# A two-block transformer kernel in one program: the third attention loop's output copies behind the exponentials, and two fill steps between scores and value products

## The chip, the cores and the metric

One core of one Trainium2 chip. The time is the device time of one execution in microseconds, for all of the work from the inputs in HBM to the output in HBM. The program is written with explicit queues: each engine (TensorE, VectorE, ScalarE, GpSimd, and SyncE for loads) has its own list of instructions, which it executes in order, and semaphores between them.

## The reference, cut to what matters

256 tokens, 1024 features, fp32. Block one (a latent and a grouped attention, an MLP, a gated embedding) and then two layers, of which the first has gated linear attention and an attention with forgetting, and the second the attention that this change touches. Each layer has two gated feed-forward halves.

```python
def odd_mixer(h, w_in, kv_norm_g, w_uk, w_uv, w_out, t5_table):
    q, ckv, q_idx, k_idx, w_idx = jnp.split(h @ w_in, ODD_SPLITS, axis=-1)
    c = rmsnorm_2(ckv, kv_norm_g)
    q_lat = jnp.einsum('bshd,hdl->bshl', q.reshape(B, S, DSA_HEADS, DSA_DH), w_uk)
    o_lat = dsa_attention(q_lat, c, ...)     # per query the best k_top keys by an index score
    o = jnp.einsum('bshl,hld->bshd', o_lat, w_uv).reshape(B, S, D_MIX_ODD)
    return o @ w_out
# in dsa_attention, for 16 heads of 64:
    s = q_lat . c_sel * DSA_DH ** -0.5 + bias(distance)      # masked where distance < 0
    p = softmax(s);  o_lat = p . c_sel
```

## The kernel before

**Matrix products.** Weights come in as chunks of 128 x 2048 fp32, in halves of 1024 columns. SyncE loads a half to `raw`; ScalarE copies it rounded to the type of TensorE's operand to `whi` (`split_half`, line 1267); VectorE writes the rest, raw minus rounded, to `wlo` (line 1715). Activations are split in the same way into a high and a low part. A product is three matmuls: high by high, high by low, low by high (`mm3`).

**The third attention loop** (`attention("odd", ...)`, one function per engine, lines 677, 1387 and 1899) works on 16 heads in 8 pairs. It has ten passes, here called rounds 0 to 9; `p` is the round. The keys and values are expanded per head beforehand, and the top-k selection is a mask that is added to the scores, so that each head is a product of 256 queries by 256 keys in two tiles: queries 0 to 127 with keys 0 to 127, queries 128 to 255 with all 256 (`OFF`, `KL`). In round p the engines do this, each in this order:

- TensorE: the scores of pair p to PSUM banks 4 and 5 (`score`, line 467 `pp<-fa`), when VectorE has reduced the pair before (`s_smax`); the value products of pair p-2 to bank 7 (`weigh`, `pp<-ptb,fa`), when ScalarE has copied that pair's turned weights (`s_ptc`) and VectorE has taken the low part of the output before (`s_ols`); fill steps (`fill(p, 0)`); the turning of head 2p-2, by transposes (`turn_weights`, line 476), when VectorE has scaled it (`s_shr`); `fill(p, 1)`; the turning of head 2p-1; `fill(p, 2)`.
- VectorE: for each of the two heads two fused operations (line 1924) that add mask and bias to the scores, write them negated to `xn`, and reduce them to the row's extreme in `st`; the low part of the output of pair p-2 (`out_lo`, line 1715 `ra<-pp,ra`), when ScalarE has written the high part (`s_ohs`); the low parts of weight halves that ScalarE split in the round before (`lows`); evictions of finished fill products (`evict`, line 1723); for each head the reciprocal of its sums (line 1952) and two scalings of the weights in `pbuf` (line 1719), when ScalarE has done the exponentials (`s_ex`).
- ScalarE: the high part of the output of pair p-2 from bank 7 (`out_hi`, line 1403, recorded at line 1267 as `ra<-pp`), when the value products are done (`s_pv`); four exponentials of pair p (line 1418); two copies of the turned weights of pair p-1 (`ptb<-pp`, line 1267); at most one weight half (`one_more`).
- GpSimd: for each head a load of a row of position biases, and two additions of it to the mask (line 2478), when VectorE has reduced the head three before.

A **fill step** is three or six matmuls of a product that has nothing to do with the pair at hand. The steps are q2 (16 steps), q3 (16), which are the queries of pairs 4 to 7, and the output projection's first half oo0.0 and oo1.0 (8 each). How many stand at which of the three places of a round comes from two tables:

```python
STEPS = {...
         "odd": {0: (7, 0, 0), 2: (3, 1, 0), 5: (3, 0, 0), 6: (2, 1, 1), 7: (2, 1, 1), 8: (2, 1, 1)}}
USUAL = {..., "odd": (3, 1, 2)}
```

q2 is thus finished in round 2 and q3 in round 5, both at the first place. VectorE's eviction of q2 (`turned_`, line 2347) is done in round 2 and that of q3 in round 5, each between the weight half and the reciprocals. The scores of round 6 wait for the eviction of q3 (`entry`, `s_qT`). Which weight halves are split in a round is fixed by how far the fill steps have come at the round's end (`ended`, `split_at`).

Of the kernel before, what the change touches and what calls it, by code (L numbers as in the profile page):

```python
# [163 lines left out]
def program(nc, W, XIN, XT, PT_IN, CST, GNS, GQK, GFIN, GFIN2, GLAG, FOXB, T5, OUT):  # L164
# [22 lines left out]
    with ExitStack() as ctx:  # L187
# [3 lines left out]
        def sem(name):  # L191
# [3 lines left out]
        ps = [pp[:, i, :] for i in range(8)]  # L195
# [36 lines left out]
        s_sc, s_smax, s_negm, s_ex, s_rcp, s_shr, s_ptn, s_ptc, s_pv, s_ohs, s_ols = [  # L232
            sem(n) for n in ("s_sc", "s_smax", "s_negm", "s_ex", "s_rcp", "s_shr", "s_ptn", "s_ptc", "s_pv",
                             "s_ohs", "s_ols")]
# [65 lines left out]
        def lo_slot(j):  # L300
# [106 lines left out]
        STEPS = {"first": {0: (9, 0, 0)}, "fox": {0: (12, 0, 0), 4: (6, 3, 3)},  # L407
                 "odd": {0: (7, 0, 0), 2: (3, 1, 0), 5: (3, 0, 0), 6: (2, 1, 1), 7: (2, 1, 1), 8: (2, 1, 1)}}
# [47 lines left out]
        def out_hi(block, j):  # L456
            return oh[:, j, :] if block == "first" else mh[:, 4 + j, :] if block == "fox" else mh[:, j, :]
# [7 lines left out]
        def tensor_program(pe):  # L465
# [211 lines left out]
            def attention(name, entry, extra, units):  # L677
                h0, pairs = HEAD0[name], COUNT[name] // 2
                off, kl = spans(name)
                causal = name != "first"  # L680
                sbk, obk = SB[name], OB[name]

                def fill(p, at):
                    point[0] = (p, at)
                    for _ in range(STEPS[name].get(p, USUAL[name])[at]):
                        next(units, None)

                def score(h, t):
                    return mm(ps[sbk[h % 2]][:, off[t]:off[t] + kl[t]], query(name, h, t), keys(name, h, kl[t]), True, True)

                def weigh(h, k):
                    o = ps[obk[h // 2 % len(obk)]][64 * (h % 2):64 * (h % 2) + 64, 0:256]
                    if causal and k == 1:
                        return mm(o[:, 128:256], values(name, h, 1), ptb[:, h % 2, 256:384], False, True)
                    return mm(o, values(name, h, k), ptb[:, h % 2, 256 * k:256 * k + 256], k == 0, k == 1)

                def turn_weights(h):
                    b = turn_bank(name, h)
                    src = weights_slot(name, h)
                    pe.wait_ge(s_shr, h0 + h + 1)  # L700
                    held = [g for g in range(h) if turn_bank(name, g) == b]
                    if held:
                        pe.wait_ge(s_ptc, h0 + held[-1] + 1)
                    elif name == "first" and b == 3:
                        pe.wait_ge(s_qbe, 3)
                    elif name == "odd" and b == 3:
                        pe.wait_ge(s_kT, 4)
                    elif name == "fox" and b == 3:
                        pe.wait_ge(s_Fout, 1)
                    for t in range(2):  # L710
                        for k in range(kl[t] // 128):
                            c = 256 * k + 128 * (t - k if causal else t)
                            y = tp(ps[b][:, c:c + 128], src[:, off[t] + 128 * k:off[t] + 128 * k + 128])
                    y.then_inc(s_ptn)

                for p in range(pairs + 2):
                    if p < pairs:
                        entry(p)
                        if p and causal:
                            pe.wait_ge(s_smax, 2 * (h0 - 16 + 2 * p))  # L720
                        elif p:
                            pe.wait_ge(s_ex, h0 + 2 * p)
                        if name == "first" and p < 4:
                            for h in (2 * p, 2 * p + 1):
                                score(h, 0)
                                score(h, 1).then_inc(s_sc)
                        else:
                            score(2 * p, 0)
                            score(2 * p + 1, 0)
                            score(2 * p, 1).then_inc(s_sc)  # L730
                            score(2 * p + 1, 1).then_inc(s_sc)
                    if p >= 2:
                        pr = p - 2
                        pe.wait_ge(s_ptc, h0 + 2 * pr + 2)
                        if pr >= len(obk):
                            pe.wait_ge(s_ols, h0 // 2 + pr + 1 - len(obk))
                        weigh(2 * pr, 0)
                        weigh(2 * pr + 1, 0)
                        weigh(2 * pr, 1).then_inc(s_pv)
                        weigh(2 * pr + 1, 1).then_inc(s_pv)  # L740
                    point[0] = (p, 0)
                    late = (name, p) == ("fox", 3)
                    if not late:
                        extra(p)
                    fill(p, 0)
                    if late:
                        extra(p)
                    ended[name, p, 0] = consumed[0]
                    if 1 <= p <= pairs:
                        turn_weights(2 * p - 2)  # L750
                        fill(p, 1)
                        turn_weights(2 * p - 1)
                        fill(p, 2)
                    ended[name, p, 1] = consumed[0]
# [509 lines left out]
        def scalar_program(act):  # L1264
            def copy(o, i, scale=None):
                if scale is None:
                    return act.activation(o, i, ACT.Copy, scale=1.0)  # L1267
                return act.activation(o, i, ACT.Copy, scale=scale)  # L1268
# [118 lines left out]
            def attention(name, evict):  # L1387
                h0, pairs = HEAD0[name], COUNT[name] // 2
                off, kl = spans(name)
                causal = name != "first"  # L1390
                sbk, obk = SB[name], OB[name]
                tot = off[1] + kl[1]

                def one_more(p, at):
                    if next_half[0] < HEND[min(ended[name, p, at] - 1 + NHL, LAST)]:
                        split_half()
                    split_at[name, p, at] = next_half[0]

                for p in range(pairs + 2):
                    if p >= 2:  # L1400
                        pr = p - 2
                        act.wait_ge(s_pv, h0 + 2 * pr + 2)
                        copy(out_hi(name, pr), ps[obk[pr % len(obk)]][:, 0:256]).then_inc(s_ohs)
                    for h in (2 * p, 2 * p + 1) if p < pairs else ():
                        hc = h0 + h
                        nm, sm, rs = head_stats(hc)
                        src = stt[:, h % 2, 0:tot] if causal else ps[sbk[h % 2]][:, 0:tot]
                        if causal:
                            act.wait_ge(s_smax, 2 * (hc - 16) + 2)
                        else:  # L1410
                            act.wait_ge(s_negm, hc + 1)
                        if h >= 4:
                            act.wait_ge(s_ptn, hc - 3)
                        if h >= 8:
                            act.wait_ge(s_shr, hc - 7)
                        o = weights_slot(name, h)
                        for t in range(2):
                            y = act.activation(o[:, off[t]:off[t] + kl[t]], src[:, off[t]:off[t] + kl[t]], ACT.Exp,
                                               bias=nm[:, t:t + 1], scale=-1.0 if causal else 1.0, accum_out=sm[:, t:t + 1])
                        y.then_inc(s_ex)  # L1420
                    evict((name, p, 0))
                    if not causal or p >= pairs:
                        one_more(p, 0)
                    if 1 <= p <= pairs:
                        for par in range(2):
                            h = 2 * p - 2 + par
                            act.wait_ge(s_ptn, h0 + h + 1)
                            if h >= 2:
                                act.wait_ge(s_pv, h0 + h - 1)
                            copy(ptb[:, par, 0:tot], ps[turn_bank(name, h)][:, 0:tot]).then_inc(s_ptc)  # L1430
                            evict((name, p, 1 + par))
                    if name == "fox" and p < pairs:
                        one_more(p, 0)
                    one_more(p, 1)
# [1164 lines left out]
```

## Time and profile before

| | |
|---|---|
| median of 3 runs | 1359.39 us (1357.41 to 1359.88) |
| profiled execution | 1357.3 us, its span 1355.3 us |
| granted TensorE clock, mean | 0.998 |
| TensorE busy (matmuls) | 1337.9 us, 99% |
| TensorE busy (weight loads) | 1147.4 us, 85% |
| VectorE busy | 969.8 us, 72% |
| ScalarE busy | 678.7 us, 50% |
| GpSimd busy | 69.6 us, 5% |

The profile is of one execution. Its times are microseconds from the start of the span; the third attention loop lies between about 1106 and 1151. A share of busy time is a mean over all stages, of which this loop is 3%. A row of a timeline gives the start, the duration, the engine, the line, the operation with its output and inputs and, in square brackets, how long the engine was idle before it and what ended that. A small overlap of successive rows of an engine is usual, as a record includes the end of the write. Where a helper records an operation, rows of many places carry its line (1267, 1715, 467), and the tile's name tells them apart.

### The profile page before, as it was taken

How to read it: one execution, taken by the hardware profiler on the slowest of the kernel's cores; microseconds unless marked ns; L12 is line 12 of the kernel's file. 1: busy time of each engine (PE TensorE's matmuls, PEld its weight loads, DVE VectorE, ACT ScalarE, POOL GpSimd, SP SyncE). 2: the span in 40 equal slices, each digit the busy share in tenths (PEclk: the TensorE clock that was granted, in tenths of full speed). 3: DMA queues.
4: the chain of work that ended last, by engine and by line, in shares of the span. 5: the costliest groups of instructions: out<-in, count | busy, mean ns of one | idle time of the engine just before them, and what ended most of it. 6: DMA issues, size and time to landing. Idle time of an engine off the chain costs nothing.

```text
span 1355.3 us, 19411 instructions
## 1 busy us (share of the span) xinstructions
PE 1337.9 (99%) x7680; PEld 1147.4 (85%) x7680; DVE 969.8 (72%) x1326; ACT 678.7 (50%) x1057; POOL 69.6 (5%) x109
## 2 busy tenths in 40 slices
PE   9999999999999999999999999999999999999998
PEld 6988888888888888898888888888888886888886
DVE  6886677666687777657667777787776798576775
ACT  6586454444554444456554443544443567544442
POOL 0300010000000000004000000000000034000000
PEclk9999999999999999999999999999999999999999
DMA  9353556555546555464446555555554554466551
GB/s 338 114 166 115 182 176 229 186 186 188 185 141 220 198 188 186 156 204 125 147 153 218 187 187 192 178 188 196 193 192 151 182 175 130 146 204 203 186 187 47
DMA packets 67594, 241.31 MB, mean 178 GB/s; under 512 B 7999, under 2 KB 8392, under 8 KB 67504
## 3 DMA queue, kind: packets, MB, share of 16 engines
q1 hardware_dynamic: 65200, 234.19, 51.9%
q0 software_dynamic: 2016, 5.77, 1.7%
q8 instruction: 61, 1.00, 0.3%
q14 instruction: 29, 0.24, 0.1%
q10 hardware_dynamic: 288, 0.11, 0.0%
HBM read 238.88 MB, written 1.09 MB: 177 GB/s over the span
## 4 chain that ended last, share of the span: by engine, by line
PE 86%; DVE 9%; ACT 2%; issue 2%; DMA 1%; POOL 0%; SPq 0%; DVEq 0%; POOLq 0%; ACTq 0%
PE pp L467 84%; DVE wlo L1715 3%; PE pp L476 2%; DVE pbuf L1719 1%; DVE fa L1715 1%; DVE xn L1924 1%; DVE hx L1723 1%; DMA raw<-w_chunks 1%; ACT whi L1267 0%; DVE fa L1815 0%; DVE fa L2294 0%; DVE xn L1715 0%; ACT hx L1268 0%; DVE st L2290 0%; DMA fa<-f_rows 0%
## 5 line engine op out<-in xcount | busy, mean ns | idle before, releaser
L1715 DVE TENSOR_TENSOR wlo<-raw,whi 128x1024 fp32r<-128x1024 f32 (+1 forms) x444 | 522.4, 1218 | 140.3 <-ACT whi L1267 140.0
L467 PE MATMUL pp<-hx,whi 128*128 128x512 f32 (+1 forms) x2400 | 541.1, 360 | 2.1 <-DVE fa L1815 1.3
L1267 ACT ACTIVATE whi<-raw 128x1024 fp32r<-128x1024 f32 (+1 forms) x444 | 441.7, 1043 | 90.6 <-PE pp L467 81.1
L467 PEld LDWEIGHTS pp<-hx,whi 128*128 128x128 f32 x2400 | 419.7, 188 | 74.3 <-issue 8.5
L467 PE MATMUL pp<-whi,ra 128*128 128x512 f32 x1144 | 366.2, 391 | 0.0
L467 PE MATMUL pp<-hx,wlo 128*128 128x256 f32 x2032 | 314.3, 278 | 0.0
L467 PEld LDWEIGHTS pp<-hx,wlo 128*128 128x128 f32 x2032 | 278.4, 188 | 9.9
L467 PEld LDWEIGHTS pp<-whi,ra 128*128 128x128 f32 x1144 | 214.6, 188 | 43.7 <-issue 0.9
L467 PE MATMUL pp<-wlo,ra 128*128 128x512 f32 x572 | 222.7, 389 | 0.0
L1815 DVE TENSOR_REDUCE fa<-pp 128x512 f32<-128x1024 f32 x104 | 126.9, 1220 | 73.4 <-PE pp L467 73.3
L1267 ACT ACTIVATE ra<-fa 128x512 fp32r<-128x512 f32 x63 | 39.8, 632 | 227.9 <-DVE fa L1723 227.9
L1363 ACT ACTIVATE fa<-fa 128x512 f32<-128x512 f32 x44 | 27.8, 632 | 195.1 <-DVE fa L1715 195.1
L467 PEld LDWEIGHTS pp<-wlo,ra 128*128 128x128 f32 x572 | 107.4, 188 | 20.3 <-issue 0.2
L467 PE MATMUL pp<-whi,hx 128*128 128x512 f32 (+2 forms) x320 | 96.0, 376 | 1.9 <-DVE wlo L1715 1.9
L1715 DVE TENSOR_TENSOR ra<-fa,ra 128x512 fp32r<-128x512 f32 x63 | 43.6, 693 | 43.3 <-ACT ra L1267 43.3
L467 PEld LDWEIGHTS pp<-whi,hx 128*128 128x128 f32 x320 | 58.4, 188 | 17.3 <-issue 6.0
L2384 POOL TENSOR_TENSOR st<-st,cst 128x2 f32<-128x2 f32 (+3 forms) x15 | 13.4, 895 | 1162.7 <-DVE st L1720 1162.7
L467 PE MATMUL pp<-wlo,hx 128*128 128x512 f32 (+2 forms) x160 | 59.4, 371 | 0.0
L1723 DVE SCALAR_TENSOR_TENSOR fa<-fa 128x512 f32<-128x512 f32 x65 | 44.4, 683 | 2.8 <-ACT fa L1614 0.7
L1723 DVE SCALAR_TENSOR_TENSOR hx<-pp,gns,hx 128x256 fp32r<-128x256 f32 x64 | 26.5, 477 | 22.9 <-ACT hx L1268 22.9
L1306 ACT ACTIVATE xn<-X 128x512 f32<-128x512 f32 x36 | 22.4, 627 | 28.3 <-DVE X L1723 28.0
L1715 DVE TENSOR_TENSOR fa<-fa,rbb 128x512 f32<-128x512 f32 x47 | 32.4, 691 | 3.5 <-ACT fa L1603 1.1
(175 smaller groups left out, 773.0 us busy)
## 6 DMA issues: line engine op xcount, KB each, us to landing
raw<-w_chunks SPq DMA_DIRECT2D x438, 512.0 KB, 5.2
fa<-t_rows POOLq DMA_DIRECT2D x16, 128.0 KB, 3.4
fx<-x_t SPq DMA_DIRECT2D x2, 512.0 KB, 6.5
X<-x_in SPq DMA_DIRECT2D x2, 512.0 KB, 7.5
fa<-g_fin POOLq DMA_DIRECT2D x2, 512.0 KB, 4.1
fa<-f_rows POOLq DMA_DIRECT2D x8, 128.0 KB, 3.2
raw<-w_chunks SPq DMA_DIRECT2D x3, 256.0 KB, 5.7
cst<-consts POOLq DMA_DIRECT2D x1, 576.0 KB, 7.5
```

Of the source, the lines that this page charges most:

```text
L467: return pe.matmul(o, lhs, rhs, start=first, stop=last, skip_group_check=True)
L476: return pe.transpose(o, src, ident[0:n, 0:n])
L1267: return act.activation(o, i, ACT.Copy, scale=1.0)
L1306: act.activation(xn[:, t, sl], X[:, t, sl], ACT.Square, scale=1.0, accum_out=st[:, q + 2 * c + t:q + 2 * c + t + 1]).then_inc(s_sq)
L1363: act.activation(fr[:, g % 2, :], fr[:, g % 2, :], ACT.Silu, scale=1.0).then_inc(s_silu)
L1715: return dve.tensor_tensor(o, a, b, op)
L1719: return dve.tensor_scalar(o, a, s1, None, op0)
L1723: return dve.scalar_tensor_tensor(out=o, in0=a, scalar=s, in1=b, op0=op0, op1=op1)
L1815: return dve.tensor_reduce(two(o), pp[:, b:b + 2, :].rearrange("p f (s c) -> p f c s", s=2), AX.X, ALU.add)
L1924: dve.tensor_tensor_reduce(out=src[:, sl], in0=bank[:, sl], in1=more[:, sl], scale=-1.0, scalar=-GONE, op0=ALU.add, op1=ALU.min, accum_out ...
L2384: return pool.tensor_tensor(o, a, C("mhalf")[:, 0:1].to_broadcast([128, n]), ALU.pow)
```

## The change

On ScalarE, in the third loop only, the copy of the output's high part (`out_copy`) stands behind the four exponentials of the round instead of ahead of them. On TensorE, in rounds 2 to 7 of the third loop only, the first two of the fill steps at the first place (of two or three) stand between the scores and the value products; the rest stay behind the value products. The other two attention loops keep their order. VectorE, GpSimd and SyncE have the same instructions in the same order.

```diff
-                def fill(p, at):
+                def fill(p, at, skip=0, most=99):
                     point[0] = (p, at)
-                    for _ in range(STEPS[name].get(p, USUAL[name])[at]):
+                    for _ in range(min(most, STEPS[name].get(p, USUAL[name])[at] - skip)):
                         next(units, None)
...
                             score(2 * p, 1).then_inc(s_sc)
                             score(2 * p + 1, 1).then_inc(s_sc)
+                    early = 2 if name == "odd" and 2 <= p < pairs else 0
+                    if early:
+                        fill(p, 0, 0, early)
                     if p >= 2:
                         pr = p - 2
                         pe.wait_ge(s_ptc, h0 + 2 * pr + 2)
...
                     if not late:
                         extra(p)
-                    fill(p, 0)
+                    fill(p, 0, early)
                     if late:
                         extra(p)
...
+                def out_copy(pr):
+                    act.wait_ge(s_pv, h0 + 2 * pr + 2)
+                    copy(out_hi(name, pr), ps[obk[pr % len(obk)]][:, 0:256]).then_inc(s_ohs)
+
                 for p in range(pairs + 2):
-                    if p >= 2:
-                        pr = p - 2
-                        act.wait_ge(s_pv, h0 + 2 * pr + 2)
-                        copy(out_hi(name, pr), ps[obk[pr % len(obk)]][:, 0:256]).then_inc(s_ohs)
+                    if p >= 2 and name != "odd":
+                        out_copy(p - 2)
                     for h in (2 * p, 2 * p + 1) if p < pairs else ():
...
                         y.then_inc(s_ex)
+                    if p >= 2 and name == "odd":
+                        out_copy(p - 2)
                     evict((name, p, 0))
```

TensorE, rounds 3 and 4: `pp<-fa` are the scores, `pp<-ptb,fa` the value products, `pp<-hx,whi` and `pp<-hx,wlo` the matmuls of fill steps, and `pp<-cst,pbuf` the turnings.

```order
 L467 MATMUL pp<-fa 128x128 x2
 L467 MATMUL pp<-fa 128x256 x2
+L467 MATMUL pp<-hx,whi 128x256 x2
+L467 MATMUL pp<-hx,wlo 128x256
+L467 MATMUL pp<-hx,whi 128x256 x2
+L467 MATMUL pp<-hx,wlo 128x256
 L467 MATMUL pp<-ptb,fa 64x256 x2
 L467 MATMUL pp<-ptb,fa 64x128 x2
 L467 MATMUL pp<-hx,whi 128x256 x2
 L467 MATMUL pp<-hx,wlo 128x256
-L467 MATMUL pp<-hx,whi 128x256 x2
-L467 MATMUL pp<-hx,wlo 128x256
```

Six matmuls, two steps, moved ahead of the value products; one step is left behind them, ahead of the first turning.

ScalarE, round 2, before: `ptb<-pp` are the copies of turned weights, `whi<-raw` a weight half, `ra<-pp` the output copy, and the rows of line 1418 the exponentials.

```order
L1267 ACTIVATE ptb<-pp 128x384 x2
L1267 ACTIVATE whi<-raw 128x1024
L1267 ACTIVATE ra<-pp 128x256
L1418 ACTIVATE pbuf,st<-xn,st 128x128
L1418 ACTIVATE pbuf,st<-xn,st 128x256
L1418 ACTIVATE pbuf,st<-xn,st 128x128
L1418 ACTIVATE pbuf,st<-xn,st 128x256
L1267 ACTIVATE ptb<-pp 128x384 x2
L1267 ACTIVATE whi<-raw 128x1024
```

ScalarE, the same round in the changed kernel (its lines 1270 and 1423 are lines 1267 and 1418 of before):

```order
L1270 ACTIVATE ptb<-pp 128x384 x2
L1270 ACTIVATE whi<-raw 128x1024
L1423 ACTIVATE pbuf,st<-xn,st 128x128
L1423 ACTIVATE pbuf,st<-xn,st 128x256
L1423 ACTIVATE pbuf,st<-xn,st 128x128
L1423 ACTIVATE pbuf,st<-xn,st 128x256
L1270 ACTIVATE ra<-pp 128x256
L1270 ACTIVATE ptb<-pp 128x384 x2
L1270 ACTIVATE whi<-raw 128x1024
```

The output copy moved from ahead of the four exponentials to between them and the copies of turned weights. It is so in each of rounds 2 to 7; rounds 8 and 9 have no exponentials.

## Rows read from the trace of the kernel before

**Rows 1.** The page, busy time of each engine with its share of the span.
```profile
PE 1337.9 (99%) x7680; PEld 1147.4 (85%) x7680; DVE 969.8 (72%) x1326; ACT 678.7 (50%) x1057; POOL 69.6 (5%) x109
```

**Rows 2.** The chain of waits from 1116 to 1136, its shares by engine and line.
```profile
by line: DVE pbuf L1719 24.3%; DVE wlo L1715 20.8%; DVE xn L1924 20.0%; issue 8.1%; ACT pbuf L1418 6.9%; PE pp L467 6.5%; DVE ra L1715 5.0%; ACT ptb L1267 3.8%; DVE fa L1723 3.0%; DVE st L1952 2.5%; DVE st L1924 0.6%; DVEq L2347 0.2%; ACTq 
```

**Rows 3.** Busy time of each engine in round 2 (length, then each engine).
```profile
1116.50:1122.30 5.80, 5.51 (x48) 4.62 (x49) 5.73 (x19) 4.31 (x13) 5.02 (x8) 1.00 0.66 210
```

**Rows 4.** Timeline of VectorE, rounds 2 to 5 (start, duration, operation).
```profile
1116.45 0.28 DVE L1924 CUSTOM_DVE_ANT_0 xn<-pp,fa 128x128 f32<-128x128 f32 x1
...
1117.56 0.41 DVE L1715 TENSOR_TENSOR ra<-pp,ra 128x256 fp32r<-128x256 f32 x1
1117.90 1.21 DVE L1715 TENSOR_TENSOR wlo<-raw,whi 128x1024 fp32r<-128x1024 f32 x1
1119.03 0.68 DVE L1723 SCALAR_TENSOR_TENSOR fa<-pp,rbb 128x512 f32<-128x512 f32 x1
...
1120.56 1.75 DVE L1719 TENSOR_SCALAR pbuf<-pbuf,st 128x128 f32<-128x128 f32 x2
1122.23 0.28 DVE L1924 CUSTOM_DVE_ANT_0 xn<-pp,fa 128x128 f32<-128x128 f32 x1
...
1123.68 1.60 DVE L1715 TENSOR_TENSOR wlo<-raw,whi 128x1024 fp32r<-128x1024 f32 x1
...
1125.39 1.04 DVE L1719 TENSOR_SCALAR pbuf<-pbuf,st 128x128 f32<-128x128 f32 x2
...
1131.76 0.28 DVE L1924 CUSTOM_DVE_ANT_0 xn<-pp,fa 128x128 f32<-128x128 f32 x1
...
1133.20 0.68 DVE L1723 SCALAR_TENSOR_TENSOR fa<-pp,rbb 128x512 f32<-128x512 f32 x1
```

**Rows 5.** Timeline of VectorE, rounds 6 to 8.
```profile
1138.84 0.55 DVE L1719 TENSOR_SCALAR pbuf<-pbuf,st 128x128 f32<-128x128 f32 x2
...
1140.49 0.29 DVE L1924 CUSTOM_DVE_ANT_0 xn<-pp,fa 128x128 f32<-128x128 f32 x1 [0.44 <-PE pp L467]
...
1146.35 0.42 DVE L1715 TENSOR_TENSOR ra<-pp,ra 128x256 fp32r<-128x256 f32 x1 [1.73 <-ACT ra L1267]
```

**Rows 6.** Timeline of TensorE's weight loads, rounds 2 to 7.
```profile
1115.53 0.63 PEld L467 LDWEIGHTS pp<-ptb,fa 128*64 128x64 f32 x8 [1.26 <-ACT ptb L1267]
...
1119.79 0.63 PEld L467 LDWEIGHTS pp<-ptb,fa 128*64 128x64 f32 x8 [0.69 <-ACT ptb L1267]
1120.59 0.30 PEld L467 LDWEIGHTS pp<-hx,whi 128*128 128x128 f32 x2 [0.17 <-issue]
...
1121.66 0.35 PEld L476 LDWEIGHTS pp<-cst,pbuf 128*128 128x128 f32 x3
...
1125.57 0.63 PEld L467 LDWEIGHTS pp<-ptb,fa 128*64 128x64 f32 x8 [1.46 <-ACT ptb L1267]
...
1130.35 0.63 PEld L467 LDWEIGHTS pp<-ptb,fa 128*64 128x64 f32 x8 [0.51 <-ACT ptb L1267]
...
1133.93 0.52 PEld L467 LDWEIGHTS pp<-fa 64*128 64x128 f32 x8 [1.03 <-DVE fa L1723]
...
1135.09 0.63 PEld L467 LDWEIGHTS pp<-ptb,fa 128*64 128x64 f32 x8 [0.63 <-ACT ptb L1267]
...
1142.45 0.48 PEld L476 LDWEIGHTS pp<-cst,pbuf 128*128 128x128 f32 x3
```

**Rows 7.** Timeline of ScalarE, round 2 and round 8.
```profile
1117.12 0.40 ACT L1418 ACTIVATE pbuf<-xn,st 128x128 f32<-128x128 f32 x1 [0.26 <-DVE st L1924]
...
1118.90 0.84 ACT L1267 ACTIVATE ptb<-pp 128x384 f32<-128x384 f32 x2
...
1145.95 0.37 ACT L1267 ACTIVATE ra<-pp 128x256 fp32r<-128x256 f32 x1
```

**Rows 8.** Timeline of GpSimd, mask additions in rounds 2 and 3.
```profile
1120.99 1.16 POOL L2478 TENSOR_TENSOR fa<-fa 128x128 f32<-128x128 f32 x2
...
1123.03 1.16 POOL L2478 TENSOR_TENSOR fa<-fa 128x128 f32<-128x128 f32 x2
```

## The prediction

> **What bounds the kernel now.** I read the page first: TensorE is busy 99% of the span [rows 1], so a change must shorten or lengthen one of its few gaps. All instructions that move lie in the third attention loop, some 44 us of the 1355.3. I number its passes as rounds 0 to 9, and use letters: S(p) the scores of pair p and V(p-2) the value products of the pair two back (TensorE), R(p) the four reductions, L the low part of a weight half, N(p) the scaling by the reciprocal sums (VectorE), E(p) the four exponentials, C(p-1) the copies of turned weights, O(p-2) the copy of the output (ScalarE), OL(p-2) the output's low part (VectorE, reads what O wrote).
>
> Then I read the chain of waits over rounds 2 to 5. It hardly touches TensorE: 6.5% against 24.3, 20.8 and 20.0% for three lines of VectorE [rows 2]. The stretches say the same: in the 5.80 us of round 2 VectorE is busy 5.73 [rows 3]. TensorE has 5.51 there, because fill steps pad it; but it is VectorE that has no hole. In the timeline of VectorE rounds 2, 3 and 5 begin at 1116.45, 1122.23 and 1131.76, each at the moment the one before ends, and no row of these has a wait [rows 4]. Only from S(6) on does TensorE set the pace: R(7) is the first to wait for it, 0.44 us [rows 5].
>
> TensorE's gaps follow from that. It waits before V: 1.26, 0.69, 1.46, 0.51, 0.63 us in rounds 2 to 6, for C; and 1.03 before S(6), for VectorE's eviction of q3 [rows 6]. The handover that carries VectorE's time to the end of the kernel is this last one: the eviction starts at 1133.20 [rows 4], S(6) at 1133.93.
>
> **The change part by part.**
>
> *Two fill steps between S and V.* Three steps run from 1120.59 to 1121.66 [rows 6], 0.36 each, so two are 0.71. They come from the same round, none is added, and all their operands are there (q2 and q3 wait only for banks long free). V starts at the later of "C done" and "S done + 0.71": of the gaps in rounds 2 to 6 up to 0.71, 0.69, 0.71, 0.51 and 0.63, in all 3.25 us, can be filled. But what follows V in TensorE's queue, the turning T(2p-2), waits for N(p-1), and S(p+1) for R(p), both VectorE's. In rounds 2 to 5 TensorE only arrives earlier where it then waits. I count nothing for them there. In round 6 TensorE leads, and its weight loads stand 0.63 before V [rows 6]; since matmuls still stream while loads stand, I take half of that, **-0.3**, with 0 and -0.63 as bounds. In rounds 8 and 9 nothing is put ahead of V.
>
> *O behind E on ScalarE.* O itself gets a place where it never makes E late. C(p-1) behind it starts some 0.3 later, which no longer matters while V has two steps ahead of it. What counts is OL. VectorE's queue is R(p), OL(p-2), L, evictions, N(p), unchanged, and OL waits for O. Before, O(p-2) was done ahead of R, and OL ran 1.11 us after the start of R (1117.56 after 1116.45 [rows 4]). Now O runs after E. From rows: first exponential 0.67 after R's start (1117.12), the four take 1.78 (C starts right behind, 1118.90 [rows 7]), and OL starts 0.40 after O does (O 1145.95 [rows 7], OL 1146.35 [rows 5], a place where it waits for it already). So OL starts 0.67 + 1.78 + 0.40 = 2.85 after R's start, not 1.11: VectorE stands **1.74 us** in each round from 2 on, with L and N queued behind it. L (1.13 us, from 1117.90 to the next start at 1119.03 [rows 4]) used to run exactly while ScalarE did the exponentials; that cover is gone.
>
> *How many rounds pay.* Rounds 2, 3 and 4 in full, and round 5 in full too, since the eviction of q3 stands behind OL(3) and S(6) waits for it. 4 x 1.74 = **+6.96**.
>
> *What the wait gives back.* N's scalings take 0.55 us a pair when nothing of GpSimd runs (1138.84 [rows 5]), 1.75 in round 2 [rows 4] and 1.04 in round 3 (the same in round 4). In round 2 a pair of GpSimd's mask additions runs beside it, from 1120.99, 1.16 us; the next pair starts 2.04 later [rows 8]. GpSimd masks a head when a head of R is done: in a slower round the first pair starts some 0.7 us after R's start, the second 2.04 later, so both are over by 0.7 + 2.04 + 1.16 = 3.9. N now starts at 2.85 + 0.34 + 1.13 = 4.3 or later. So I take the slow part off: 1.75 - 0.55 = 1.20 in round 2, 0.49 in rounds 3 and 4: **-2.18**, with 0 as the other bound. In return L of round 2 may fall beside a mask, as that of round 3 did (1.60 against 1.21 [rows 4]): **+0.39**, bounds 0 and 0.39. The Trainium skill says of this, in "SBUF — State Buffer", section Who interferes with whom, that a VectorE scaling in its two-port mode and a GpSimd instruction lock each other out for a whole instruction, whoever is first; by it the relief is whole wherever N and masks no longer meet, and none where they still do. The rows fit this, 0.55 against 1.04 and more.
>
> *Rounds 6 and 7.* VectorE arrives 1.74 late at N(6), but T(12) at 1142.45 [rows 6] stands 3.06 behind N's first scaling (1139.39 [rows 5]): covered. In round 7 R first loses its 0.44 wait, then OL is late again: some 1.74 - 0.44 + 1.6 = 2.9 late at N(7), against a like cover of 3 us. So nothing, up to 0.6 if it is missed.
>
> *Sum:* 6.96 - 2.18 + 0.39 - 0.3 = **+4.87**, call it 4.9. The bounds: relief 0 and 0.6 in round 7 give 6.96 + 0.39 + 0.6 = +8; all relief, no slower L and 0.63 gained at V give +4.1. I take the relief in full because the places of the masks are known from R. The profiled execution (1357.3 us, span 1355.3) would become 1362.2; it lies at the low end of the three times, so against their median of 1359.39 the forecast is **1364.3 us**. Weight loads and splits don't enter: their order is unchanged.
>
> **The rivals.**
>
> *A, faster: TensorE's own gaps are the bound.* Then the steps fill 3.25 us and O's place costs nothing: 1356.1. It needs VectorE to have 1.74 us of slack in each round. For it: 99% on TensorE, and VectorE's 1.74 might fall in gaps the rows hide. Against it: 5.73 busy of 5.80. The Trainium skill's "Perfetto Trace Analysis", Identifying the Most-Contended Engine and Optimization Strategy, has one optimize the engine of the highest occupancy and close its gaps first; followed by the whole-kernel share, that is this rival. 7%.
>
> *B, no difference to speak of: only the last wait counts.* If rounds 2 to 4 absorb the delay (masks, scalings and exponentials regroup by more than I took off) and only round 5's wait before S(6) reaches TensorE, 1.74 - 0.3 = 1.4: 1360.8. For it: the chain has 8.1% of "issue" in rounds 2 to 5, and the contended instructions are large. 17%.
>
> *C, worse: nothing is given back and round 7 is missed.* GpSimd's masks also move with R and meet L and N again, and N(7) and C(6) come behind T(14) and V(6): +8 to +10, 1367.4 to 1369.4. It decides from 3 us of delay at N(7). 10%.
>
> That the copies and steps don't move as described is excluded by the order of both kernels.
>
> **How the numbers follow.** Forecast 66%, A 7%, B 17%, C 10%. 0.2% of this kernel, about what a measurement can tell from no change, is 2.7 us: faster means under 1356.7, slower over 1362.1. The forecast's own range (+4.1 to +8) is 1363.5 to 1367.4. To hold 8 in 10 the range takes in most of B and of C: 1359.5 to 1368.5; A and the tails stay out. Faster 0.07 (A), within 0.17 (B), slower 0.76 (forecast and C).
>
> **What the profile of the changed kernel would show.** VectorE idle about 1.7 us before OL in each of rounds 2 to 6, released by ScalarE's O, where there was no wait; a bit less in round 7. Rounds 3 and 4 of some 6 us instead of 4.8. TensorE's gaps before V gone or under 0.7 in rounds 2 to 6, and in their place waits before the turnings for N, and some 1.7 more before S(6) relative to R(5). N's scalings at 0.55 instead of 1.04 to 1.75. The loop, from S(2) to the last V, longer by 4 to 5 us, and all before and after it as it was. I am wrong if VectorE doesn't stand before OL, or if it does and S(6) comes less than 3 us later than before.

## The result, and the profile after

| | before | changed |
|---|---|---|
| median | 1358.4 us (1356.94 to 1359.88, 4 runs) | 1366.31 us (1364.86 to 1369.47, 4 runs) |
| profiled execution, its span | 1357.3, 1355.3 us | 1366.53, 1364.5 us |
| granted clock, mean | 0.998 | 0.995 |

The change makes the kernel slower: the ratio is 1.0064, 95% interval 1.0051 to 1.0077, that is 8.7 us (6.9 to 10.5), where 4.9 were forecast. The time measured lies inside the range, the sign is right, and the size was underrated by more than a third. The page, in answer to [rows 1]:

```profile
PE 1342.9 (98%) x7680; PEld 1149.7 (84%) x7680; DVE 967.6 (71%) x1326; ACT 678.1 (50%) x1057; POOL 68.8 (5%) x109
```

The same number of instructions, VectorE 2 us less busy, and TensorE 5 us more. The loop is best read in three stretches: from the scores of round 0 to those of round 6, from there to the scores of round 7, and from there to the last value products. First the kernel before, then the changed one (start and end, length, busy time of TensorE, weight loads, VectorE, ScalarE and GpSimd, granted clock, DMA share, GB/s):

```profile
1106.39:1133.93 27.54, 24.43 (x207) 19.95 (x206) 27.19 (x93) 20.25 (x65) 21.38 (x36) 1.00 0.64 177
1133.93:1139.53 5.60, 5.37 (x34) 3.75 (x35) 5.46 (x21) 5.24 (x17) 2.01 (x4) 1.00 0.02 5
1139.53:1149.42 9.89, 9.89 (x61) 6.89 (x60) 7.21 (x21) 7.11 (x17) 0.00 (x0) 1.00 0.36 113
```
```profile
1107.85:1140.72 32.87, 26.09 (x208) 20.29 (x207) 25.94 (x93) 21.23 (x69) 21.49 (x37) 0.98 0.58 149
1140.72:1148.53 7.81, 7.81 (x34) 5.04 (x34) 4.02 (x17) 3.90 (x13) 1.15 (x2) 0.66 0.00 0
1148.53:1158.57 10.04, 10.04 (x62) 6.83 (x61) 7.78 (x24) 7.10 (x17) 0.00 (x0) 1.00 0.36 116
```

The first stretch is 5.33 us longer, the second 2.21, the third 0.15: 7.69 in all. VectorE had 0.35 us idle in the first stretch before and has 6.93 now. The rest of the 9.2 us between the two spans lies ahead of the loop, where both kernels execute the same instructions: the loop began 1.46 us later. In the first 20 us of this execution TensorE's mean clock was 0.91 instead of 1.00. That start is seen in five of the thirteen traces of this case, whose loops begin at 1107.56 to 1108.20, and not in seven others, whose loops begin at 1105.91 to 1106.51 (one begins at 1108.62 with a full clock there); why an execution starts one way or the other is open. Behind the loop both kernels take the same time (205.9 us).

The timeline of VectorE in the changed kernel, in answer to [rows 4] (its lines 1722, 1726 and 1730 are 1715, 1719 and 1723 of before):

```profile
1117.93 0.28 DVE L1931 CUSTOM_DVE_ANT_0 xn<-pp,fa 128x128 f32<-128x128 f32 x1
...
1120.76 0.42 DVE L1722 TENSOR_TENSOR ra<-pp,ra 128x256 fp32r<-128x256 f32 x1 [1.64 <-ACT ra L1270]
...
1124.24 0.29 DVE L1931 CUSTOM_DVE_ANT_0 xn<-pp,fa 128x128 f32<-128x128 f32 x1
...
1127.08 0.42 DVE L1722 TENSOR_TENSOR ra<-pp,ra 128x256 fp32r<-128x256 f32 x1 [1.64 <-ACT ra L1270]
1127.42 1.88 DVE L1722 TENSOR_TENSOR wlo<-raw,whi 128x1024 fp32r<-128x1024 f32 x1
...
1129.40 0.55 DVE L1726 TENSOR_SCALAR pbuf<-pbuf,st 128x128 f32<-128x128 f32 x2
...
1139.64 0.42 DVE L1722 TENSOR_TENSOR ra<-pp,ra 128x256 fp32r<-128x256 f32 x1 [1.64 <-ACT ra L1270]
1139.98 0.68 DVE L1730 SCALAR_TENSOR_TENSOR fa<-pp,rbb 128x512 f32<-128x512 f32 x1
...
1146.89 0.42 DVE L1722 TENSOR_TENSOR ra<-pp,ra 128x256 fp32r<-128x256 f32 x1 [3.29 <-ACT ra L1270]
```

Each of rounds 2 to 5 has a hole of 1.64 us ahead of the output's low part, released by ScalarE's copy (1.65 in round 4); so has round 7. In round 6 the hole is 3.29 us, as the copy there waits for value products that come late. The low part starts 2.83 us after the reductions (1120.76 after 1117.93; the forecast had 2.85). The scalings of rounds 3 and 4 are down to 0.55, and the weight half of these rounds went up to 1.88. Weight loads of TensorE, in answer to [rows 6]:

```profile
1127.84 0.63 PEld L467 LDWEIGHTS pp<-ptb,fa 128*64 128x64 f32 x8 [0.62 <-ACT ptb L1270]
...
1130.01 0.31 PEld L476 LDWEIGHTS pp<-cst,pbuf 128*128 128x128 f32 x3 [0.95 <-DVE pbuf L1726]
...
1140.72 0.93 PEld L467 LDWEIGHTS pp<-fa 64*128 64x128 f32 x8 [3.46 <-DVE fa L1730]
...
1148.53 0.52 PEld L467 LDWEIGHTS pp<-fa 64*128 64x128 f32 x8 [0.36 <-issue]
```

The wait before the value products of round 4 is 0.62 instead of 1.46, but 0.95 stands before the turning behind them, for VectorE's scalings. Before the scores of round 6 it is 3.46 us instead of 1.03. And these scores' loads take 0.93 instead of 0.52: the clock fell. The same columns as above, in steps of 1 us:

```profile
1138.00:1139.00 1.00, 0.00 (x0) 0.00 (x0) 0.00 (x1) 1.00 (x5) 1.00 (x3) 1.00 0.76 311
1139.00:1140.00 1.00, 0.00 (x0) 0.00 (x0) 0.36 (x2) 1.00 (x5) 0.83 (x2) 0.56 0.10 41
1140.00:1141.00 1.00, 0.28 (x2) 0.28 (x4) 0.96 (x5) 1.00 (x2) 0.00 (x0) 0.50 0.00 0
...
1145.00:1146.00 1.00, 1.00 (x5) 0.53 (x6) 0.00 (x0) 0.00 (x0) 0.00 (x0) 0.52 0.00 0
1146.00:1147.00 1.00, 1.00 (x11) 0.77 (x8) 0.11 (x1) 0.47 (x2) 0.00 (x0) 1.00 0.00 0
```

While TensorE stood idle its clock went to 0.50, the level of 1.2 GHz, and it stayed there until 1146, through the scores, the first steps and the value products of round 6. That is the second stretch, and it holds 2.44 of TensorE's 5.0 us of additional busy time (7.81 against 5.37). Another 1.66 stand in the first stretch, all of it before the clock fell, so it is not the clock's, and I did not trace it further. No part of the forecast had the fall of the clock.

### The profile page after: what moved, and what is told of

Its sections match the earlier page's. It is cut to its first block, busy times and chain, and to the rows that moved or that the text cites. A ratio compares the mean times of both kernels' runs of the same rounds, so it can differ in the third digit from the quotient of the medians.

```text
span 1364.5 us, 19411 instructions
## 1 busy us (share of the span) xinstructions
PE 1342.9 (98%) x7680; PEld 1149.7 (84%) x7680; DVE 967.6 (71%) x1326; ACT 678.1 (50%) x1057; POOL 68.8 (5%) x109
## 4 chain that ended last, share of the span: by engine, by line
PE 86%; DVE 9%; ACT 2%; issue 2%; DMA 1%; POOL 0%; DVEq 0%; POOLq 0%; SPq 0%; ACTq 0%
PE pp L467 84%; DVE wlo L1722 3%; PE pp L476 2%; DVE fa L1722 1%; DVE pbuf L1726 1%; DVE hx L1730 1%; DVE xn L1931 1%; ACT pbuf L1423 0%; DMA raw<-w_chunks 0%; ACT whi L1270 0%; DVE fa L1822 0%; DVE fa L2301 0%; DVE xn L1722 0%; ACT hx L1271 0%; DVE st L2297 0%
## 5 line engine op out<-in xcount | busy, mean ns | idle before, releaser
L467 PEld LDWEIGHTS pp<-wlo,hx 128*128 128x128 f32 x160 | 30.5, 191 | 5.7
```

Source lines behind the costliest of these rows:

```text
L467: return pe.matmul(o, lhs, rhs, start=first, stop=last, skip_group_check=True)
```

## The experiments

The theory after the result: VectorE's wait for the late copy costs the first stretch its 5.3 us, the gap that it leaves on TensorE costs the second its 2.2 us through the clock, and the two fill steps do next to nothing. The rival: the steps, or a path other than VectorE's wait, are behind it. All times below are ratios against runs of the kernel before on the same chip; "us" from a ratio is of 1358.4.

**One part alone.** The copy behind the exponentials without the steps:

```diff
-                    early = 2 if name == "odd" and 2 <= p < pairs else 0
+                    early = 0
```

> The output copy behind the exponentials, no fill step ahead of the value products. My theory (VectorE stands before the output's low part because the copy now comes after the exponentials; the gap this leaves on TensorE before the scores of round 6 then drops its clock): nearly all of the loss is here: VectorE waits 1.6 us in each of rounds 2 to 5, the scores of round 6 come 5 us later counted from the scores of round 0, a stretch at 1.2 GHz behind them, +7 to +9 us against the kernel before. Rival (the fill steps ahead of the value products hold up the turnings and copies, and the copy is harmless): within 1.5 us of the kernel before.

1.0059 (1.0046 to 1.0073), as slow as the whole change. Scores 0 to 6 in 32.84 us, 6 to 7 in 8.17. Its weight loads:

```profile
1127.58 0.63 PEld L467 LDWEIGHTS pp<-ptb,fa 128*64 128x64 f32 x8 [1.74 <-ACT ptb L1270]
1129.75 0.31 PEld L476 LDWEIGHTS pp<-cst,pbuf 128*128 128x128 f32 x3 [0.24 <-DVE pbuf L1726]
...
1140.45 0.93 PEld L467 LDWEIGHTS pp<-fa 64*128 64x128 f32 x8 [3.46 <-DVE fa L1730]
```

Without the steps the wait before the value products is 1.74 and that before the turning 0.24; with them it was 0.62 and 0.95, and the stretch took as long (32.87 us). They only moved TensorE's waiting from one place to the next. The steps without the copy's move (the edit is shown against the kernel before, and the steps are those of the change):

```diff
                 for p in range(pairs + 2):
                     if p >= 2:
-                        pr = p - 2
-                        act.wait_ge(s_pv, h0 + 2 * pr + 2)
-                        copy(out_hi(name, pr), ps[obk[pr % len(obk)]][:, 0:256]).then_inc(s_ohs)
+                        out_copy(p - 2)
```

> Two fill steps ahead of the value products, the output copy where it was. My theory: TensorE only arrives earlier where VectorE then holds it; nothing waits longer in rounds 2 to 5, at most 0.6 us is gained in rounds 6 and 7, where the copy may hold the exponentials by up to 1 us under a cover of 3: -0.6 to +0.5 us, clock full. Rival (the steps are the cause): +5 to +8 us. A second rival (TensorE's gaps before the value products were the bound): -3 us.

1.0008 (0.9999 to 1.0017): at most a small loss. Scores 0 to 6 in 27.55 us, as before (27.54). But from there to the last value products it takes 16.35 instead of 15.49. The copy now waits for later value products and holds the exponentials of rounds 6 and 7, where TensorE leads, and before the value products of round 8 there is a new wait of 1.24 us (the first row is the scores of round 6, whose wait was 1.03):

```profile
1135.11 0.52 PEld L467 LDWEIGHTS pp<-fa 64*128 64x128 f32 x8 [1.69 <-DVE fa L1728]
1146.86 0.63 PEld L467 LDWEIGHTS pp<-ptb,fa 128*64 128x64 f32 x8 [1.24 <-ACT ptb L1270]
```

So the loss is the copy's, and the steps bring nothing. In rounds 6 and 7, where they stand ahead of the value products, either the copy is late or the exponentials are.

**The clock.** The whole change, with matmuls of constants in TensorE's gap before the scores of round 6. They add work whose results nobody reads; there were six in the first kernel and three in the second.

```diff
                     if p == 6:
+                        for _ in range(6):
+                            mm(ps[2][:, :], C("ones"), C("hot"), True, True)
                         pe.wait_ge(s_qT, 4)
```

> The change whole, and six matmuls of constants (128x512, results unused) ahead of TensorE's wait before the scores of round 6, in its gap of 3.5 us. They leave that wait's end where it is. My theory (the clock fell because of that gap, and the half clock costs 2.2 us behind it): granted clock 1.00 through round 6, scores of round 6 to scores of round 7 in 5.6 us instead of 7.8, +5.3 to +6.2 us against the kernel before instead of +7.9. Rival (the longer round 6 is a consequence of the late VectorE, whatever the clock): no shorter than the change, +7 to +9.

1.0050 (1.0037 to 1.0062), that is 6.8 us (5.0 to 8.4), more than I expected and too wide to tell the theory from its rival. The six took 5.32 us, more than the gap, and the scores of round 6 came 1.86 us later than in the change (34.73 us after those of round 0). Scores 6 to 7 took 5.44 us, at full clock. With three:

> The change whole, with three matmuls of constants (128x512, results unused) in TensorE's gap before the scores of round 6; six of them took 5.32 us and pushed those scores 1.9 us back, three take 2.7 and fit into the gap of 3.5. My theory (half clock behind the gap costs 2.2 us): scores of round 0 to scores of round 6 in 32.9 us as in the change, scores of round 6 to 7 in 5.5 us at a granted clock of 1.00, +5.0 to +6.2 us against the kernel before. Rival (the clock is only a sign, the time comes from late VectorE work): +7 to +9.

```profile
1108.62:1141.48 32.86, 28.63 (x213) 21.29 (x212) 25.93 (x93) 21.23 (x69) 21.58 (x37) 1.00 0.57 149
1141.48:1146.95 5.47, 5.47 (x35) 3.68 (x35) 3.75 (x16) 3.69 (x13) 1.14 (x2) 1.00 0.00 0
1146.95:1156.99 10.04, 10.04 (x61) 6.81 (x60) 7.87 (x26) 7.11 (x17) 0.00 (x0) 1.00 0.35 117
```

The first stretch is that of the change to 0.01 us, the second 5.47 instead of 7.81, at full clock. In all 1.0041 (1.0028 to 1.0055), 5.6 us. The difference of 2.34 us in the second stretch is the price of the clock, with all the rest equal; it is read from the stretches, since the intervals of the two whole times still overlap. Kernels with such added work are no improvement, since the gap itself stays. The Trainium skill, in "TensorE: Matmul & The Clock Gate", section HAM oscillation, describes this, a gap that throttles the clock and a stretch of work behind it that pays; the trace agrees, at 0.50 from 1140 to 1145.

**VectorE's wait taken away.** The change whole, with the low part moved in VectorE's queue, so that the weight half covers the exponentials again. First behind the scalings:

```diff
-                    if p >= 2:
-                        pr = p - 2
+                    def out_low(pr):
                         dve.wait_ge(s_ohs, h0 // 2 + pr + 1)
...
+                    last_low = name == "odd" and 2 <= p < pairs
+                    if p >= 2 and not last_low:
+                        out_low(p - 2)
...
                         y.then_inc(s_shr)
+                    if last_low:
+                        out_low(p - 2)
```

> The change whole, but VectorE takes the output's low part at the end of its round, behind the scalings, so that it no longer stands waiting for the copy. My theory: the waits of 1.6 us go, the weight half again covers the exponentials, the scores of round 6 come as early as before or 0.3 us earlier (the eviction of q3 no longer has the low part ahead of it), full clock: 0 to -1.2 us against the kernel before. Rival (the copy's lateness costs through another path, the copies of turned weights or the steps): +4 us or more stay.

1.0029 (1.0019 to 1.0040), 3.9 us (2.6 to 5.4): not the gain that I expected, and by the whole time alone the rival could stand. The stretches decide: scores 0 to 6 take 27.51 us, as before, so the 5.3 us are gone. But the first step of the output projection in round 6 waits for the low part of pair 3, now at the end of round 5, and the clock fell behind that gap. Scores 6 to 7 took 8.71 us:

```profile
1136.36 0.50 PE L467 MATMUL pp<-whi,ra 128*128 128x512 f32 x1 [1.69 <-DVE ra L1722]
```
```profile
1137.00:1138.00 1.00, 1.00 (x4) 0.80 (x3) 1.00 (x5) 1.00 (x5) 1.00 (x2) 0.52 0.00 0
```

The same with round 5 apart, where the low part goes right behind the eviction of q3 (the difference from the kernel above, where `moved` is its `last_low`):

```diff
                     if not states:
                         evict((name, p, 0))
+                    if moved and p == 5:
+                        out_low(p - 2)
...
-                    if last_low:
+                    if moved and p != 5:
                         out_low(p - 2)
```

> The change whole; VectorE takes the output's low part at the end of its round, but in round 5 right behind the eviction of q3, so that the fill steps of round 6, which wait for it, find it done. My theory: no wait before it in rounds 2 to 4, scores of round 0 to 6 in 27.2 us (27.5 before), no gap, full clock, -0.2 to -1.2 us against the kernel before. Rival (more than VectorE's wait is behind the loss): +2 us or more.

1.0014 (1.0005 to 1.0022), where no loss was expected. Scores 0 to 6 take 29.48 us, 6 to 7 take 5.43. The cause is again a wait that my edit put in. The value products of round 3 wait for the low part of pair 0 (they share bank 7), and at the end of round 2 it is late. In the profiled execution this left a gap of 2.76 us and half clock from 1123 to 1127:

```profile
1122.58 0.88 PE L467 MATMUL pp<-ptb,fa 128*64 128x256 f32 x8 [2.76 <-DVE ra L1722]
```
```profile
1122.00:1123.00 1.00, 0.42 (x4) 0.40 (x6) 1.00 (x7) 0.00 (x0) 0.57 (x1) 1.00 0.62 217
1123.00:1124.00 1.00, 1.00 (x10) 0.79 (x5) 1.00 (x5) 0.98 (x5) 0.86 (x2) 0.66 0.34 70
1124.00:1125.00 1.00, 1.00 (x6) 1.00 (x6) 0.96 (x3) 1.00 (x6) 1.00 (x1) 0.50 0.38 70
```

Up to this place the kernel is the same as that of the first order, whose trace has this wait too, 2.13 us long. There the clock stayed at 1.00 and the first stretch took 27.51 us, so most of the 2 us between 27.51 and 29.48 go with this fall of the clock. The row of the first order:

```profile
1121.71 0.87 PE L467 MATMUL pp<-ptb,fa 128*64 128x256 f32 x8 [2.13 <-DVE ra L1722]
```

Then in the middle of the round, behind the weight half and the evictions and ahead of the scalings:

```diff
                         evict((name, p, 0))
-                    if moved and p == 5:
+                    if moved:
                         out_low(p - 2)
...
-                    if moved and p != 5:
-                        out_low(p - 2)
```

> The change whole; VectorE takes the output's low part behind the weight half and the evictions, ahead of the scalings, in all of rounds 2 to 7. There it is late enough not to wait long for the copy and early enough for the value products of the next round, which waited for it in the last two orders. My theory: waits before it of 0 to 0.6 us in rounds 2 to 4 instead of 1.64, scores of round 0 to 6 in 27.3 to 28.5 us, no gap over 3 us on TensorE, clock 1.00, and +0.3 to +1.7 us in all. Rival (the wait of VectorE is not the cause): +4 us or more.

1.0023 (1.0014 to 1.0033), 3.1 us (1.9 to 4.5), above my range of 0.3 to 1.7; the interval just holds the rival's 4. Scores 0 to 6 take 28.79 us, 1.25 more than before and 0.3 above what I expected, and the clock is whole. VectorE's waits are of the size expected, and two of TensorE's follow them (VectorE, then TensorE):

```profile
1126.57 0.42 DVE L1722 TENSOR_TENSOR ra<-pp,ra 128x256 fp32r<-128x256 f32 x1 [0.47 <-ACT ra L1270]
...
1132.29 0.42 DVE L1722 TENSOR_TENSOR ra<-pp,ra 128x256 fp32r<-128x256 f32 x1 [0.50 <-ACT ra L1270]
```
```profile
1137.00 0.93 PE L467 MATMUL pp<-fa 64*128 64x128 f32 x8 [1.16 <-DVE fa L1730]
1138.46 0.50 PE L467 MATMUL pp<-whi,ra 128*128 128x512 f32 x1 [0.54 <-DVE ra L1722]
```

The loop as a whole is 44.89 us against 43.03 before and 50.72 in the change. Some 1.2 us of the measured 3.1 are not seen in the loop of the one profiled execution, whose span is 3.6 us longer than that of before because its loop also began 1.81 us later; how much of the 1.2 is such a start stays open. With three places for one instruction, which shorten the first stretch from 32.87 us to 27.51, 29.48 and 28.79, VectorE's wait as its cause is shown. None of the three is better than the kernel before: in each the late low part makes somebody wait.

**What VectorE's queue is worth.** The last experiments start from the kernel before. Weight halves are split later, none in the first rounds of the loop. `held` is rounds 0 to 3 here, and 0 to 4 in the last two kernels:

```diff
                 def one_more(p, at):
-                    if next_half[0] < HEND[min(ended[name, p, at] - 1 + NHL, LAST)]:
+                    held = name == "odd" and p in (0, 1, 2, 3)
+                    if not held and next_half[0] < HEND[min(ended[name, p, at] - 1 + NHL, LAST)]:
```

> The kernel before; ScalarE splits no weight half in rounds 0 to 3 of the third loop, so VectorE has four low parts of 1.1 to 1.6 us less in rounds 1 to 4; they follow later by the same rule. My theory (VectorE's queue sets rounds 1 to 5): scores of round 0 to 6 in 24 to 26 us instead of 27.5, and -1.5 to -3.5 us in all if the later halves are absorbed. Rival (TensorE's own gaps or the loop over all engines set the rounds): 27 us, no gain; or the gain is given back where the weights come late.

1.0000 (0.9991 to 1.0008), no gain where 1.5 to 3.5 us were expected. Four low parts of weights less, and scores 0 to 6 still take 27.46 us. The theory "VectorE's work sets the rounds" was too simple. Without the halves a round takes 4.24 us (reductions at 1121.80, 1126.04), which is what GpSimd needs for its two masks with a load ahead of each. The chain of waits from 1117 to 1131 runs mainly over GpSimd (masks 54.3%, their loads 15.4%):

```profile
by line: POOL fa L2479 54.3%; POOL fa L2469 15.4%; DVE xn L1925 13.4%; issue 11.3%; DVE pbuf L1720 6.9%; POOLq L2476 0.6%; DVE st L1925 0.5%
```

And the scalings that run beside the masks are stretched, to 1.56 us where a pair takes 0.55 elsewhere:

```profile
1122.58 1.15 POOL L2479 TENSOR_TENSOR fa<-fa 128x128 f32<-128x128 f32 x2 [0.21 <-DVE st L1925]
...
1124.61 1.15 POOL L2479 TENSOR_TENSOR fa<-fa 128x128 f32<-128x128 f32 x2
...
1126.82 1.14 POOL L2479 TENSOR_TENSOR fa<-fa 128x128 f32<-128x128 f32 x2 [0.20 <-DVE st L1925]
```
```profile
1124.56 1.56 DVE L1720 TENSOR_SCALAR pbuf<-pbuf,st 128x128 f32<-128x128 f32 x2
...
1131.82 1.47 DVE L1716 TENSOR_TENSOR wlo<-raw,whi 128x1024 fp32r<-128x1024 f32 x1
1133.21 0.68 DVE L1724 SCALAR_TENSOR_TENSOR fa<-pp,rbb 128x512 f32<-128x512 f32 x1
```

What was left of the gain (round 5 began 1.6 us earlier, counted from the scores of round 0) went to the half of round 4, which now stood ahead of the eviction of q3 for 1.4 us. The same on top of the second order of low parts:

> e6 and e7 together: the change, the low part at the end of the round, no weight half split in rounds 0 to 3. My theory: with VectorE relieved, TensorE's gaps before the value products come into play and the two steps fill them: 0.5 to 1.5 us better than e7, -2 to -5 us against the kernel before. Rival: no better than e7.

1.0008 (0.9999 to 1.0017), not better than the one before it, where a gain of 2 to 5 us was expected; scores 0 to 6 in 27.47 us. Then the half of round 4 was held too:

> The kernel before; no weight half split in rounds 0 to 4 of the third loop (e7 held 0 to 3, and the half of round 4 then stood ahead of the eviction of q3, 1.47 us, which gave back what rounds 3 and 4 had gained; there GpSimd's pair of masks, 4.1 us, set the rounds). My theory: scores of round 0 to 6 in 25.8 to 26.6 us, -0.8 to -2 us in all. Rival: given back later, within 0.5 us of the kernel before.

```profile
1106.31:1132.89 26.58, 24.37 (x207) 19.96 (x207) 24.74 (x89) 16.42 (x62) 20.87 (x37) 1.00 0.46 105
1132.89:1138.29 5.40, 5.37 (x34) 3.75 (x35) 5.26 (x22) 4.96 (x17) 1.44 (x3) 1.00 0.04 8
1138.29:1148.18 9.89, 9.89 (x61) 6.89 (x60) 6.84 (x20) 7.21 (x18) 0.00 (x0) 1.00 0.37 116
```

0.9987 (0.9979 to 0.9996): 1.8 us faster than the kernel before (0.5 to 2.9), the first version that is, and as far as expected. With the two steps ahead of the value products in rounds 2 to 5:

> As e10, with the two fill steps ahead of the value products in rounds 2 to 5 alone (in rounds 6 and 7 they held the output copy and through it the exponentials, 1.24 us before the value products of round 8), the copy ahead of the exponentials. My theory: TensorE's gaps there are not the bound, within 0.5 us of e10. Rival (with VectorE relieved the gaps count): 0.7 us or more better than e10.

0.9989 (0.9980 to 0.9998), the same as without them: also where VectorE is relieved TensorE's gaps before the value products are not the bound.

## Why the prediction was right or wrong, point by point

**The bound.** Right in the place, too narrow in the cause. VectorE had no hole and each hole put into it came out at TensorE. But right behind VectorE stands GpSimd: with four weight halves taken out the rounds did not get shorter than about 4.24 us, and the chain went over GpSimd's masks.

**The two fill steps.** Right: nothing in rounds 2 to 5, and the waits before the turnings of 0.95 us appeared as said. The -0.3 for round 6 can't be read from the change, whose round 6 ran at half clock. With the clock kept the second stretch is 5.47 us instead of 5.60, so 0.13 came of it. It went again in the third: that takes 10.04 or 10.05 us in all seven kernels that have the late copy and the steps in rounds 6 and 7, and 9.89 or 9.90 in the five without steps there. By themselves, with the copy ahead of the exponentials, the steps cost 0.9 us from round 6 on, since the copy then holds the exponentials. That was not considered, as in the change the copy is out of the way.

**The copy.** Right: the low part starts 2.83 us after the reductions (2.85 forecast). The rounds from 2 to 5 begin 6.31, 6.29 and 6.28 us apart, at 1117.93, 1124.24, 1130.53 and 1136.81. With [rows 4] the three were 15.31 us and are 18.88, 3.57 more; by the working it was 3 x 1.74 - 2.18 + 0.39 = 3.43. In round 5 the eviction comes 3.17 us after the reductions instead of 1.44, 1.73 more. Together 5.30 of the 5.33 measured.

**Relief and price beside GpSimd.** Taken together it was right to 0.14 us, in its parts less so: the scalings of rounds 3 and 4 fell to 0.55 as said, but the weight half of these rounds rose from 1.60 to 1.88, so what the scalings no longer paid the weight half partly did. It starts at 1127.42, beside a pair of masks that began at 1127.05. In round 2 it stayed at 1.21: it started behind the masks, and the next pair, which began while it ran, took 1.38 instead of 1.15:

```profile
1121.94 1.38 POOL L2485 TENSOR_TENSOR fa<-fa 128x128 f32<-128x128 f32 x2
...
1127.05 1.15 POOL L2485 TENSOR_TENSOR fa<-fa 128x128 f32<-128x128 f32 x2
```

So in both places the one that starts second gets longer, though no run sets this apart. It fits what the Trainium skill says in "SBUF — State Buffer", section Who interferes with whom: a scaling in the two-port mode and a GpSimd instruction lock each other out, whoever is first, and an operation of VectorE with two inputs in SBUF, as the weight half is, contends with GpSimd instructions that read SBUF.

**Rounds 6 and 7.** Right for their cover: the third stretch is 0.15 us longer, which goes with the steps and not with the copy (above), though VectorE stood 3.29 us before its low part in round 6 and 1.64 in round 7. The sign "the loop longer by 4 to 5 us" failed, it was 7.69.

**What was missing** is a term of the sum: the clock behind the gap before the scores of round 6. The gap itself follows from the forecast's own numbers. The eviction starts 1.74 us later while TensorE has nothing to do but wait; the wait of 1.03 [rows 6] was bound to grow, and was 3.46. The forecast counted a gap at its length alone. It also cost 2.2 us behind it (7.81 instead of 5.60), measured by itself as 2.34. With this term 4.87 would have been 7.1 to 7.2, against 7.69 in the loop and 6.9 to 10.5 in all. That the time measured also lies inside the forecast's own bounds (+4.1 to +8, 1363.5 to 1367.4) is luck: their upper end was made of a relief that fails and a round 7 that is missed, and neither happened.

**The rivals.** A (faster) fell with the result and with the steps alone at 1.0008; B (only the last wait counts) fell with rounds 2 to 4, 3.57 us longer. C had about the right size and the wrong mechanism: the relief came and its round 7 was covered.

## What to carry to other kernels

Before an instruction is moved back in one engine's queue, look at who reads its result and what is queued behind that reader: here one copy of 0.4 us, moved behind 1.8 us of exponentials, cost 5.3 us by way of an engine that the diff does not touch. Filling gaps of the busiest engine brought nothing while another engine set the round; ask first what would be late next. And a gap on TensorE is to be priced with what follows it: behind gaps of 1.7 to 3.2 us, though not behind each of them, the work here ran at half clock, and took some 2 us more where that was measured.

## What was not expected of the hardware

The granted clock fell to 0.50 at idle stretches of TensorE of quite different length: 3.22 us in the changed kernel, where it fell some 1.6 us into the gap; 2.76 in round 3 of one order of the low parts and only 1.69 in round 6 of another, where it fell 0.7 to 0.8 us after the matmuls had begun again. But an idle stretch of 2.13 us, in round 3 of the latter kernel, left it whole. So the length of a gap alone does not tell here whether the clock falls, and the wait of round 3, 2.13 us in one trace and 2.76 in the other, met both outcomes in kernels that are the same up to there. Gaps of 1.16 and 0.54 us close to each other left it whole too, as did those up to 1.06 of the kernel before. The clock was back at 1.00 some 6.8 us after it had fallen in the changed kernel and 3.4 us after in the two others. The six matmuls of 128x512 fp32 constants took 5.32 us, 0.89 each: I had expected all six to fit into the gap of 3.5 us, which spoiled the first of the two clock experiments.
